# Expert layer: first products as three one-pass products, one-hot keys on ScalarE, gathered rows in the place of x and h

## The reference, cut to what matters

```
def peer(h, w_q, subkeys, u, v):
...
        ids = jnp.take_along_axis(cand_id.reshape(C, PEER_HEADS, PEER_TOPK * PEER_TOPK), pos, axis=-1)
        g = jax.nn.softmax(best, axis=-1)
        ue = jnp.take(u, ids, axis=0)
        ve = jnp.take(v, ids, axis=0)
        a = jax.nn.gelu(jnp.einsum('cd,chkd->chk', xc, ue), approximate=False)
        return jnp.einsum('chk,chkd->cd', (g * a).astype(xc.dtype), ve)
```

## Time and profile before

| What | us |
|---|---|
| median of 3 runs | 4017.27 |
| lowest and highest run | 4007.2, 4031.96 |
| the profiled execution, its own time | 4011.07 |
| its span in the profile | 4009.2 |
| prologue of the expert layer, first gates product to up(0) | 2780.0 to 2899.1 |
| steps 0 to 95 (with gates) | 2899.1 to about 3735 |
| steps 96 to 127 (tail) | to 3968.5 |
| sum into x, last norm, store | to 4009.2 |

### The profile page before, as it was taken

One profiled execution on the slowest core, in us unless ns is written; L12 is line 12 of the kernel. 1 busy time (PEld: TensorE's weight loads), 2 busy tenths in 40 slices (PEclk: granted clock), 3 DMA queues, 4 the chain that ended last, 5 costly groups with the idle time before them and its releaser, 6 DMA issues. The chain is left out here.

```text
span 4009.2 us, 41696 instructions
## 1 busy us (share of the span) xinstructions
PE 3438.9 (86%) x15124; PEld 2495.1 (62%) x15124; DVE 2021.2 (50%) x3660; ACT 892.2 (22%) x1339; POOL 865.3 (22%) x756
## 2 busy tenths in 40 slices
PE   6789879897969879986778988463999999999997
PEld 4645658775735558864157645343977777777664
DVE  3136333323136433321164442798777777777666
ACT  2134333212233333311033432210100000000001
POOL 0020100000020100000000210001666555666553
PEclk8868889998968889998989889776599999999998
DMA  3420122222330023223515111112599999999996
GB/s 119 144 59 1 32 74 94 88 101 77 112 109 1 18 72 94 89 101 110 215 68 153 36 33 47 54 37 89 155 326 347 349 346 350 340 352 347 385 409 252
DMA packets 204935, 620.01 MB, mean 155 GB/s; under 512 B 31296, under 2 KB 64864, under 8 KB 200544
## 3 DMA queue, kind: packets, MB, share of 16 engines
q1 hardware_dynamic: 131040, 349.37, 25.5%
q0 software_dynamic: 73728, 268.47, 18.2%
HBM read 596.92 MB, written 18.74 MB: 154 GB/s over the span
## 5 line engine op out<-in xcount | busy, mean ns | idle before, releaser
L109 PE MATMUL psum<-sbuf 128*128 128x512 f32 (+1 forms) x1680 | 677.3, 403 | 253.5 <-DVE sbuf L1808 98.3
L110 PE MATMUL psum<-sbuf 128*128 128x512 f32 (+1 forms) x1680 | 662.6, 394 | 0.0
L111 PE MATMUL psum<-sbuf 128*128 128x512 f32 (+1 forms) x1680 | 661.2, 394 | 0.0
L109 PEld LDWEIGHTS psum<-sbuf 128*128 128x128 f32 x1680 | 324.0, 193 | 335.9 <-DVE sbuf L1808 100.3
L2040 PE MATMUL psum<-sbuf 128*128 128x512 f32 x1024 | 472.4, 604 | 6.0 <-DVE sbuf L2154 6.0
L2031 PE MATMUL psum<-sbuf 128*128 128x256 f32 x2048 | 464.7, 380 | 0.0
L2031 PEld LDWEIGHTS psum<-sbuf 128*128 128x128 f32 x2048 | 390.2, 191 | 107.0 <-issue 60.3
L1044 POOL TENSOR_TENSOR sbuf<-sbuf 64x768 fp32r<-64x768 f32 (+2 forms) x22 | 29.2, 1326 | 1831.7 <-ACT sbuf L990 1831.7
L110 PEld LDWEIGHTS psum<-sbuf 128*128 128x128 f32 x1680 | 324.6, 193 | 70.4 <-issue 5.0
L111 PEld LDWEIGHTS psum<-sbuf 128*128 128x128 f32 x1680 | 323.4, 192 | 68.2
L1997 POOL DMA_INDIRECT sbuf<-peer_u,sbuf x256 | 324.5, 1268 | 121.1 <-DVE sbuf L2123 68.0
(11 more groups left out here) (267 smaller groups left out, 4451.2 us busy)
## 6 DMA issues: line engine op xcount, KB each, us to landing
sbuf<-peer_ut SPq DMA_DIRECT2D x128, 512.0 KB
sbuf<-peer_v SPq DMA_DIRECT2D x128, 512.0 KB
sbuf<-w_ffn SPq DMA_DIRECT2D x88, 512.0 KB, 3.5
sbuf<-w_mod SPq DMA_DIRECT2D x12, 2048.0 KB
sbuf<-w_down SPq DMA_DIRECT2D x16, 1408.0 KB, 5.8
sbuf<-w_fm SPq DMA_DIRECT2D x38, 512.0 KB, 4.5
sbuf<-w_out SPq DMA_DIRECT2D x24, 512.0 KB, 3.5
sbuf<-w_tm SPq DMA_DIRECT2D x10, 1024.0 KB, 5.9
```

The lines of the kernel that those rows point to most:

```text
L109: nc.tensor.matmul(acc, w_high(k), x_high(k), start=(k == 0), stop=False)
L110: nc.tensor.matmul(acc, w_high(k), x_low(k), start=False, stop=False)
L111: mm = nc.tensor.matmul(acc, w_low(k), x_high(k), start=False, stop=(k == kt - 1))
```

## The change

The stage keeps its steps and its rings. What is different:

- **up(s)** is three one-pass products in place of one 32-bit product: the `ut` tile is split into a high part (ScalarE, `split_u`, L2103) and the rest (VectorE, `split_u`, L2218), h into `h_high` and `h_low` once at the start, and `split_products` makes high x high, high x low and low x high: 24 products of 256 columns. The split of tile s + 2 stands in step s, on ScalarE behind the gelu and on VectorE between w(s) and the rows.
- **Gates** are one-pass products. The weight is split in two (`halved`), `part` has 64 columns for each token, and the two halves of the result are added: ScalarE copies the first (L2122), VectorE adds the second (`take`, L2180).
- **hot** is made by ScalarE in all 96 steps with gates and in every second group of the prologue: eight squares of (iota - key) and one relu(1 - square) (L2111, L2114). VectorE makes it in the others.
- **Rows** are gathered into `xT` and `hT`, four ring places in each. x is stored to memory before (`x_kept`, 2 MB) and loaded back after row 507 has been used.
- SyncE's load of ut tile s waits for the split of tile s - 3 in the place of up(s - 3).

```diff
-def peer_experts(nc, C, hT, h_tok, stream, ids, weights, ut, u, v, u_in, y):
+def peer_experts(nc, C, xT, hT, h_tok, stream, ids, weights, ut, u, v, u_in, y, x_d):
...
+    h_dense = hT[:, :, tok0:S]
+    rows = [(xT, hT)[r // 4][:, r % 4 * 2:r % 4 * 2 + 2, :].rearrange("p k s -> p (k s)") for r in range(RING)]
...
+    def on_act(n):
+
+        return n >= GROUPS or n % 2 == 1
...
-        rows, odd = sb([P, RING, D]), sb([P, D])
+        odd = sb([P, D])
+        u_high, u_low = sb([P, 2, D], F32R), sb([P, 2, D], F32R)
+        h_high, h_low = sb([P, KT, DENSE], F32R), sb([P, KT, DENSE], F32R)
         v_in = sb([P, HELD, D])
         gate = sb([P, 2, QUARTER, DENSE])
-        hot, part, equal = sb([P, 2, GROUP, NKEY]), sb([P, 2, GROUP, QUARTER]), sb([P, GROUP, QUARTER])
-        picked = sb([P, 3, DENSE])
+        hot, equal = sb([P, 2, GROUP, NKEY], F32R), sb([P, GROUP, QUARTER])
+        part = sb([P, 2, GROUP, 2, QUARTER], F32R)
+        picked, halved = sb([P, 3, DENSE]), sb([P, DENSE, 2], F32R)
...
         def _(sp):
+            sp.dma_start(x_d, xT[:, :, :].rearrange("p k s -> p (k s)")).then_inc(x_stored, 16)
             for s in range(NKEY):
                 if s >= HELD:
-                    sp.wait_ge(a_made, s - HELD + 1)
+                    sp.wait_ge(u_low_made, s - HELD + 1)
                 sp.dma_start(u_in[:, s % HELD, :], ut[s]).then_inc(u_landed[s % HELD], 16)
                 if s >= HELD:
                     sp.wait_ge(y_made, s - HELD + 1)
                 sp.dma_start(v_in[:, s % HELD, :], v[s * P:(s + 1) * P, :]).then_inc(v_landed[s % HELD], 16)
+            sp.wait_ge(x_stored, 16)
+            for n in range(ROWS - RING, ROWS - RING // 2):
+                wait_row(sp, n)
+            sp.dma_start(xT[:, :, :].rearrange("p k s -> p (k s)"), x_d).then_inc(x_back, 16)
+            sp.wait_ge(x_back, 16)
...
-                pool.wait_ge(hot_made, 2 * n + 2)
-                nc.gpsimd.tensor_tensor(part[:, n % 2, :, :], equal[:, :, :],
-                                        picked[:, 2, toks].unsqueeze(2).to_broadcast([P, GROUP, QUARTER]), ALU.mult
-                                        ).then_inc(parts_made, 1)
+                pool.wait_ge(equal_made, n + 1)
+                nc.gpsimd.tensor_tensor(part[:, n % 2, :, :, :],
+                                        equal[:, :, :].unsqueeze(2).to_broadcast([P, GROUP, 2, QUARTER]),
+                                        halved[:, toks, :].bitcast(F32).unsqueeze(3).to_broadcast([P, GROUP, 2, QUARTER]),
+                                        ALU.mult).then_inc(parts_made, 1)
...
+                    elif n < RING // 2:
+                        pool.wait_ge(x_stored, 16)
+                    else:
+                        pool.wait_ge(h_low_made, 1)
+                    pool.indirect_dma_start(rows[n % RING], None, (u, v)[f],
                                             bass.IndirectOffsetOnAxis(ap=stream[:, t, j:j + 1], axis=0)
                                             ).then_inc(gathered[n % RING], 16)
...
             def gates(n):
-                pe.wait_ge(hot_made, 2 * n + 2)
+                if on_act(n):
+                    pe.wait_ge(one_made, squares(n) + 1)
+                else:
+                    pe.wait_ge(own_made, n - squares(n) + 1)
                 pe.wait_ge(parts_made, n + 1)
                 if n >= 2:
                     pe.wait_ge(gates_taken, n - 1)
                 for j in range(GROUP):
-                    mm = nc.tensor.matmul(g_ps[:, n % 2, j * QUARTER:(j + 1) * QUARTER], hot[:, n % 2, j, :],
-                                          part[:, n % 2, j, :], start=True, stop=True)
+                    mm = nc.tensor.matmul(g_ps[:, n % 2, 2 * j * QUARTER:2 * (j + 1) * QUARTER], hot[:, n % 2, j, :],
+                                          part[:, n % 2, j, :, :], start=True, stop=True)
                 mm.then_inc(gates_made, 1)
 
             def up(s):
                 if s < 2:
                     pe.wait_ge(copied, 2)
+                    pe.wait_ge(h_low_made, 1)
                 else:
                     pe.wait_ge(gelu_done, s - 1)
-                pe.wait_ge(u_landed[s % HELD], 16 * (s // HELD + 1))
-                for k in range(KT):
-                    mm = nc.tensor.matmul(a_ps[:, s % 2, 0:DENSE], u_in[:, s % HELD, k * P:(k + 1) * P], hT[:, k, tok0:S],
-                                          start=(k == 0), stop=(k == KT - 1))
-                mm.then_inc(a_made, 1)
+                pe.wait_ge(u_low_made, s + 1)
+                split_products(nc, a_ps[:, s % 2, 0:DENSE], KT, lambda k: u_high[:, s % 2, k * P:(k + 1) * P],
+                               lambda k: u_low[:, s % 2, k * P:(k + 1) * P], lambda k: h_high[:, k, :],
+                               lambda k: h_low[:, k, :]).then_inc(a_made, 1)
...
+            nc.scalar.activation(halved[:, :, 0], picked[:, 2, :], ACT.Copy).then_inc(high_made, 1)
+            nc.scalar.activation(h_high[:, :, :], h_dense, ACT.Copy).then_inc(h_high_made, 1)
+
+            def split_u(s):
+                act.wait_ge(u_landed[s % HELD], 16 * (s // HELD + 1))
+                nc.scalar.activation(u_high[:, s % 2, :], u_in[:, s % HELD, :], ACT.Copy).then_inc(u_high_made, 1)
+
+            def one_hot(n):
+
+                if n >= 2:
+                    act.wait_ge(gates_made, n - 1)
+                for j in range(GROUP):
+                    at = n % GROUPS * GROUP + j
+                    nc.scalar.activation(hot[:, n % 2, j, :], C.iota[:, :], ACT.Square, bias=picked[:, 1, at:at + 1],
+                                         scale=-1.0).then_inc(squared, 1)
+                act.wait_ge(squared, GROUP * (squares(n) + 1))
+                nc.scalar.activation(hot[:, n % 2, :, :], hot[:, n % 2, :, :].bitcast(F32), ACT.Relu, bias=C.ones[:, 0:1],
+                                     scale=-1.0).then_inc(one_made, 1)
...
+            for s in range(2):
+                split_u(s)
             for n in range(GROUPS):
+                if on_act(n):
+                    one_hot(n)
                 take(n)
                 gelu_dots(n - GROUPS)
             for s in range(NKEY):
+                if s + GROUPS < QUARTERS * GROUPS and on_act(s + GROUPS):
+                    one_hot(s + GROUPS)
                 act.wait_ge(a_made, s + 1)
                 if s >= 2:
                     act.wait_ge(w_made, s - 1)
                 nc.scalar.activation(act_out[:, s % 2, :], a_ps[:, s % 2, 0:DENSE], ACT.Gelu).then_inc(gelu_done, 1)
+                if s + 2 < NKEY:
+                    split_u(s + 2)
                 if s + GROUPS < QUARTERS * GROUPS:
...
             def one_hot(n):
                 q, g = n // GROUPS, n % GROUPS
-                if n >= 2:
-                    dve.wait_ge(gates_made, n - 1)
                 toks = slice(g * GROUP, (g + 1) * GROUP)
-                nc.vector.tensor_tensor(hot[:, n % 2, :, :], C.iota[:, :].unsqueeze(1).to_broadcast([P, GROUP, NKEY]),
-                                        picked[:, 1, toks].unsqueeze(2).to_broadcast([P, GROUP, NKEY]),
-                                        ALU.is_equal).then_inc(hot_made, 1)
+                if not on_act(n):
+                    if n >= 2:
+                        dve.wait_ge(gates_made, n - 1)
+                    nc.vector.tensor_tensor(hot[:, n % 2, :, :], C.iota[:, :].unsqueeze(1).to_broadcast([P, GROUP, NKEY]),
+                                            picked[:, 1, toks].unsqueeze(2).to_broadcast([P, GROUP, NKEY]),
+                                            ALU.is_equal).then_inc(own_made, 1)
                 if n:
                     dve.wait_ge(parts_made, n)
                 nc.vector.tensor_tensor(equal[:, :, :], C.iota[:, q * QUARTER:(q + 1) * QUARTER].unsqueeze(1)
                                         .to_broadcast([P, GROUP, QUARTER]),
                                         picked[:, 0, toks].unsqueeze(2).to_broadcast([P, GROUP, QUARTER]),
-                                        ALU.is_equal).then_inc(hot_made, 1)
+                                        ALU.is_equal).then_inc(equal_made, 1)
+
+            def take(n):
+
+                q, g = n // GROUPS, n % GROUPS
+                dve.wait_ge(gates_begun, n + 1)
+                place = gate[:, q % 2, :, g * GROUP:(g + 1) * GROUP]
+                nc.vector.tensor_tensor(place, g_ps[:, n % 2, :].rearrange("p (t x i) -> p x i t", t=GROUP, x=2)[:, 1, :, :],
+                                        place, ALU.add).then_inc(gates_taken, 1)
...
+            def split_u(s):
+                dve.wait_ge(u_high_made, s + 1)
+                if s >= 2:
+                    dve.wait_ge(a_made, s - 1)
+                nc.vector.tensor_tensor(u_low[:, s % 2, :], u_in[:, s % HELD, :], u_high[:, s % 2, :].bitcast(F32),
+                                        ALU.subtract).then_inc(u_low_made, 1)
+
             dve.wait_ge(copied, 2)
+            dve.wait_ge(h_high_made, 1)
```

(12 more changed lines are left out.)

25 lines of the change are left out of this document (17 added, 8 removed).

## The result

| | us |
|---|---|
| before, median of 4 runs beside the changed kernel | 4012.72 (4007.2 to 4031.96) |
| changed kernel, median of 4 runs | 4351.71 (4346.74 to 4355.58) |
| ratio, 95% interval | 1.0835 (1.0795 to 1.0874) |
| span of the profiled execution, before and after | 4009.2, 4344.9 |

The changed kernel is 8.35% slower. The forecast was 4200 us, the range 3995 to 4370. The measured time lies inside the range, though nearer to its upper end than to the forecast.

The account below looks back on a forecast made before the run. It took PE as the limit in steps with gates (8.67 us a step), DMA close behind. 4011 + 11 (start) + 8 (prologue) + 171 (chain) + 0 (tail) + 2 (end) = 4203, forecast 4200 us, range 3995 to 4370.

Parts of the forecast that it names:

- the chain: Loop of waits through five engines, down(k) to down(k + 2), in steps with gates: 20.9 us per two steps, +171 us.
- Steps 7 and 8: Last links of the two-step loop, TensorE's gates and down: 0.85 and 3.68 us.
- the clock as a rival: TensorE's clock falls in its waits, down and gates take twice as long: 2.3 us a step more, 4420 us; chance 0.10.
- Step 1: First link of the loop: from issue of the v and ut loads to the last packet, 7.5 us (7.0 to 8.0).
- Step 4: Link of the loop: VectorE's rows behind the low part, 3.75 of them in 4.5 us.
- Step 6: Link of the loop: GpSimd's part, grown from 256 to 512 columns, 1.3 us (0.82 to 1.5).
- the prologue: Groups of gates before the 96 steps: 3.7 us a group against 3.45, +8 us (-15 to +30).
- the tail: Last steps, without gates: DMA stays the limit, change 0 us (-5 to +10).
- ScalarE's round: Rival in steps with gates: only ScalarE's loop of landing, split, take, one-hot, gates, down binds; 8.5 us a step, 4016 us; chance 0.07.
- The start: VectorE's first one-hot must wait for h's low part and two split ut tiles, which stand behind x: +11 us.
- the end: Behind the last steps: x is loaded back only once row 507 is used, +2 us.
- The chain does not form: Rival in steps with gates: the products' saving comes through, a step is DMA's 7.5 us, 3920 us; chance 0.13.

Follow-up runs that it names:

- e11_no_gathers: Changed kernel without the gathers of rows 120 to 511, so it computes something else: 4178.9 us, ratio 1.0423 to the kernel before.
- e2: Changed kernel with VectorE's low part of tile s + 2 made behind the rows of step s, not ahead: 4108.93 us, ratio 1.0226 to the kernel before.
- e6: Changed kernel with equal and part of group s + 33 made ahead of the rows of step s: 4161.31 us, ratio 1.0385 to the kernel before.
- e7_all_ahead: Changed kernel with the edits of e1_u_ahead and e6, all prologue one-hots on VectorE, x stored behind the first two ut tiles: 3933.51 us, ratio 0.9815.
- e1_u_ahead: Changed kernel with SyncE's loads of ut issued one place earlier, ut(s + 3) after v(s): 4044.88 us, ratio 1.0068 to the kernel before.
- e3_fill: Changed kernel with up's 24 products made a second time in each step with gates, result thrown away: 4286.76 us, ratio 1.0668 to the kernel before.

## Why the prediction was right, and where its sizes were off

The direction and the mechanism held: the chain is there, link by link, and three cuts in it give time back. The size was short by nearly half: +336 us between the spans for a forecast of +192. The forecast gave 20.9 us for a turn of two steps. The turn shown above, and the mean of the 45 turns from 2963.90 to 4046.07, by those steps:

| step | forecast | this turn | mean of 45 |
|---|---|---|---|
| 1 landing | 7.5 | 9.64 | 8.37 |
| 2 ScalarE's split | 1.06 | 1.09 with its hand-over | 1.09 |
| 3 VectorE's low part | 1.22 | 1.14 | 1.16 |
| 4 rows | 4.5 (3.75 of them) | 3.59 (3 of them) | 4.04 (3 or 4, mean 3.5) |
| 5 equal | 0.42 | 0.56 with its hand-over | 0.67 |
| 6 part | 1.3 | 1.05 | 1.05 |
| 7 gates | 0.85 | 1.70, and 0.10 ahead of it | 1.68, and 0.10 |
| 8 down | 3.68 | 5.34, and 0.02 behind it | 5.86, and 0.03 |
| sum | 20.9 with 0.4 of hand-overs | 24.23 | 24.05 |

- **Steps 7 and 8** are the term that was mis-sized most: 1.68 + 5.86 for 0.85 + 3.68, 3.0 us a turn, 1.5 a step, 144 us in all. I had them at full clock and kept the clock as a rival at 0.10 that excludes the forecast. It doesn't exclude it: the chain makes PE wait, the clock falls in the wait, and the slow products are in the chain. The rival was priced at 2.3 a step for all products at the half clock; only the step of a pair that had waited had it. The Trainium skill's page "TensorE: Matmul & The Clock Gate" says that idle gaps between bursts let the clock fall; by that rule this rival would be the likely one, and the trace agrees, here behind a wait of 7.14 us, and behind 2.20 in e11_no_gathers.
- **My reason against it** was that PE would wait 3 us in every 10. The mean is about right, (1150 - 842) / 96 = 3.2 a step, but it comes as one wait of 3.8 to 8.9 us (mean 6.5) in every second step. I followed the chain of two steps and then spoke of each step as if it were alone.
- **Step 1** was read from one load of the kernel before, 7.0 to 8.0. The mean in the changed kernel is 8.37, 0.9 more a turn, 42 us in all. Alone the two tiles take 4.9 (e11_no_gathers), so gathers make 3.6 of the median of 8.5. The other value that stood beside mine, 8.2, worked out from the Trainium skill's page "DMA: Bandwidth & Descriptors" (each DMA engine takes turns between its queues), was the nearer one. That is partly luck. It is 5.2 us for the bytes and 3.0 for a start that the prediction gives no source for, and a share of one half is not what the trace shows in each microsecond: SP's queue moved 0.35 MB and the rows none in 3303:3304, then 0.04 and 0.36 in 3306:3307.
- **Step 4** was too long: the chain's steps use 3 or 4 rows, 3.5 on the average and not 3.75, which is 0.46 less a turn, -22 us. **Step 6** took 1.05 for my 1.3, -12 us. Its lower bound of 0.82 was an average over two kinds: in the kernel before, L1984 takes 0.62 in the steps with gates and 1.46 in most of the prologue, where it runs beside VectorE.
- What is left, equal with its hand-over and the other hand-overs against the 0.4 allowed, is -2 us. Together 171 + 144 + 42 - 22 - 12 - 2 = 321, against 3.33 x 96 = 320 measured.
- **The range held by a margin that was not meant.** A turn of 24.05 is longer than the forecast's own upper end, 23.8, and +320 more than its +310. With the central values of the other terms that end gives 4342; 4351.7 lies inside 4370 because the upper ends of the prologue (+30) and the tail (+10) were added in, and neither was reached. It is nearer to the rival's 4420 than to the forecast's 4200.
- **The signs.** Of those that were to show the forecast right, the wait of L2218 for L2103 and of that for the DMA of `ut` came, gates released by GpSimd too, but in every second step; the tail came nearly (7.5 us a step for 7.2, 399 GB/s). Steps of 10 to 11 us did not (12.04), nor DMA near 290 GB/s (249). And one of the signs of being wrong came, PEclk well below 1.0 from 2900 us on: 0.80.
- **ScalarE's round** (8.5 a step) did not bind in the changed kernel: in the turn above its one-hot ended 2.6 us ahead of GpSimd's part. But it stood close under the chain, and with the rows out, in e2 and e6, gates waited for it. Eight squares took 2.43 and the relu 1.15, 3.6 in all for the 3.4 forecast. Gates of 64 columns take 0.82 for eight at full clock, forecast 0.85.
- **The start** +12.6 for +11, **the prologue** +10 for +8 (3.83 us a group for 3.7), **the tail** +6 for 0, inside -5 to +10, **the end** -1 for +2. The start's 1.9 us until the first packet stands in no row; in the kernel before, the first packet of SP's queue begins 0.96 us after the first issue at 2775.36.
- "The chain does not form", 3920 us, is what e7_all_ahead came near (3933.5) once SyncE's and VectorE's orders were changed. Its condition, a tile asked for a step earlier, was named rightly; e1_u_ahead shows that it was not enough by itself.

## What to carry to other kernels

When an operand gets a preparing step ahead of its use, move its load by as much in the queue's own list, and look at what that list puts in front of it. Follow a new wait through the whole loop until it meets itself, then follow the next shortest loop too, since that is what is left when the first is cut. Where TensorE stands in such a loop with waits of 3 us and more, price the products behind the wait at the half clock: all 252 such waits in these runs were followed by a slow down. And look at how the waits fall on the steps, not at their mean.

## What the runs showed of the hardware

- In the steps with gates of the changed kernel and the eleven others (1128 steps), a down took either 3.68 us or 4.95 to 6.63. Which one went with TensorE's wait ahead of the gates in front of it: none of 724 downs was slow behind a wait under 1 us, all 252 were behind 3 us and more, and 104 of 152 in between; the shortest wait with a slow down was 1.14 us, the longest without one 2.70. The gates behind these 252 waits were slow too (1.3 us and more for eight products, 1.70 as a rule; 0.8 to 1.0 otherwise) in 231. What the engine did before such a wait was not varied. More work for the engine made the kernel faster (e3_fill).
- VectorE's w, 128 x 256 with both inputs in SBUF, took 0.42 us in all 48 steps in which it did not overlap GpSimd's part, and 1.23 (median) in the 48 in which it did (3315.45 beside 3315.34); part was unhurt at 1.05. In e7_all_ahead part beside the rows took 1.46, and the two kinds of rows 1.58 and 1.68 beside part, 1.22 and 1.28 without it, as in the earlier trace rows.
- Two tiles of 512 KB took 4.9 us from issue to use with no gathers about, 8.5 with them, and the chain shortened by the whole difference.
